# Prompt sparse attention: value products in the two PSUM halves, probability sums on Pool

## The chip, the cores and the metric

The kernel runs on one core of a Trainium2 chip. The metric is the device time of one execution in microseconds (us). The core's engines work side by side and meet at semaphores: TensorE (PE, matrix products into the eight banks ps of PSUM; PEld are its weight loads), VectorE (DVE), ScalarE (ACT), GpSimd (POOL) and SyncE (SP, here for transfers). Pool cannot read PSUM.

## The reference

One inference step of a hybrid decoder layer for a prompt group of 1024 tokens and a sample group of 8 x 4 tokens: input projection, RWKV-7 mixing, causal pooling, sparse attention, merging, cross-attention to 256 memory tokens, and an MLP. The change touches the sparse attention of the prompt alone. It has 8 query heads of 64 in 2 kv groups (4 heads share the keys and values of a group) and three branches:

```
lc = q . kc * scale + bias; pc = masked_softmax(lc);  o_cmp = pc . vc   # 16 block means
ls = q . ks * scale + bias; ps = masked_softmax(ls);  o_slc = ps . vs   # selected blocks of 64
lw = q . kw * scale + bias; pw = masked_softmax(lw);  o_win = pw . vw   # window of 512 keys
o = gate0 * o_cmp + gate1 * o_slc + gate2 * o_win
```

The prompt has 16 blocks and 16 are selected, so the selected branch sees every key up to the query's own position. The window branch sees the last 512. Both softmaxes need, for each query and head, a maximum, a sum of the exponentials and the product of the exponentials with the values.

## The kernel before, in words

The kernel is a chain of stages, each a block with one written program for each engine; a stage starts when the one before it has ended on all engines. `stage_nsa_prompt` is one of them. Its work is cut into 16 units: query tile i (128 tokens, i = 0 to 7) times kv group g, unit u = 2i + g. A unit has "tiles" of 128 keys: i + 1 of kind "s" (selected) and min(i, 4) + 1 of kind "w" (window), 2 to 13 a unit, 132 in all. G counts tiles over all units, k within one.

For a tile, `scores(G)` on TensorE writes 128 keys x (4 heads x 128 queries) into bank G % 2 with two products: L2152 (high parts of the keys) and L2153 (low parts, and a row that subtracts the maximum). Near the diagonal and at the window's edge, VectorE (`biased`, L2286) adds a bias into the ring PT, `np_probsT`, of four slots (NPT), and ScalarE takes the exponential there (L2357); for the other tiles ScalarE reads the bank itself (L2362). Two tiles later `values(G)` on TensorE (L2164) multiplies with the values, in plain fp32. The values have a 65th column of ones, so that row 64 of the result is the sum of the exponentials. Selected tiles add up in bank 2, window tiles in bank 3.

The rest of a unit is woven between the tiles of the next one by `plan(u)`. `look(u + 1, c)` computes scores the other way round for the maxima of the next unit (L2124, and L2120 for the edge; the form "cmp" at L2114 gives the scores of the block means), and VectorE's `see` reduces them (L2249, L2253). Looks use banks 4 and 5 in turn: look C waits until look C - 2 is seen. The form "cmpT" (L2117) turns the weights of the block means after VectorE's chain L2260 to L2267. `shift` (L2134) turns the negated maxima, in bank 7. After a unit's last tiles ScalarE evacuates both sums of products into OT (L2374), `turn` transposes them into banks 6 and 7 (L2173), VectorE's `scale` divides by the sums and multiplies by the gates (L2293 to L2299), `final` turns back and adds the block-mean branch (L2183, L2184), and `final_out` on ScalarE stores into oC (L2383). Pool only issues one gather at the stage's start (L2441).

Other places in the kernel are named by the prediction: L3608 in the cross-attention of the samples (`sample_values`: for each of four batches two products with 32 weight columns, into partitions 32b to 32b + 31 of one bank), L2617 and L2609 in the sample attention (a product with 32 weight columns, and transposes), L799, L811 and L816 in the RWKV preparation, and L1398 and L1942, elementwise work of Pool.

## Time and profile before

| | |
|---|---|
| time, median of 3 runs | 3045.2 us (3043.39 to 3047.57) |
| time of the profiled execution | 3039.11 us |
| its span | 3036.9 us |
| busy over the span | PE 2730.9, PEld 2440.2, DVE 1156.6, ACT 795.2, POOL 163.7 us |
| stage of the change | from 994.7 to 1343.6 us of the span: 348.9 us |
| mean granted TensorE clock | 0.94 of full over the span, 0.92 in the stage |

The span is the part of the profiled execution between its first and last instruction; 2.2 us lie around it. Times within the trace are counted from the span's start. A "record" is one line of TensorE's trace; an fp32 product has two, each with a weight load of its own. Record lengths overlap, because TensorE is a pipeline: the distance between two starts is what a record costs.

### The profile page before, as it was taken

What the parts mean: (1) busy time and instruction counts of PE and PEld (TensorE: products, weight loads), DVE (VectorE), ACT (ScalarE), POOL (GpSimd) and SP (SyncE); (2) the same over time, 40 slices, a digit from 0 to 9 for tenths busy, and PEclk for the clock granted to TensorE, in tenths of its full rate; (3) what the DMA queues carried; (4) which work ended last, traced back from release to release, by engine and by line L of the source; (5) the groups of instructions that cost most, each with busy time, mean ns of one, the idle gap of its engine ahead of it and who ended that gap; (6) DMA issues with size and microseconds to landing.
All of it is one profiled execution on the core that took longest, in us unless ns stands there. A gap on an engine that the chain in (4) does not pass through costs nothing. (4 is left out here: it accounts for less than half of the span.)

```text
span 3036.9 us, 49131 instructions
## 1 busy us (share of the span) xinstructions
PE 2730.9 (90%) x21538; PEld 2440.2 (80%) x21538; DVE 1156.6 (38%) x2020; ACT 795.2 (26%) x1245; POOL 163.7 (5%) x215
## 2 busy tenths in 40 slices
PE   5898588887997789987899999999889999999999
PEld 4897488873996455553689999999679999999998
DVE  4433644426052555634421333433444222222223
ACT  3223322211114334432221221221433212222112
POOL 1000222201211000012000000000000000000000
PEclk7999799987998699998999999998989999999999
DMA  4610100004530000027611111401301111111111
GB/s 164 235 42 15 17 3 3 3 4 149 114 86 4 18 1 1 1 104 253 264 46 49 46 42 53 126 26 35 118 21 49 43 49 49 42 49 42 49 49 65
DMA packets 178933, 192.09 MB, mean 63 GB/s; under 512 B 18214, under 2 KB 162897, under 8 KB 173624
## 3 DMA queue, kind: packets, MB, share of 16 engines
q1 hardware_dynamic: 168665, 127.05, 14.2%
q0 software_dynamic: 9888, 61.87, 5.9%
q8 instruction: 170, 2.79, 0.4%
q14 instruction: 42, 0.34, 0.0%
q10 hardware_dynamic: 168, 0.04, 0.0%
HBM read 165.28 MB, written 28.00 MB: 64 GB/s over the span
## 5 line engine op out<-in xcount | busy, mean ns | idle before, releaser
L3386 PE MATMUL ps<-ff_hidden_high,ff_high 128*128 128x352 f32 x768 | 247.7, 323 | 0.0
L3387 PE MATMUL ps<-ff_hidden_low,ff_high 128*128 128x352 f32 x768 | 246.7, 321 | 0.0
L3388 PE MATMUL ps<-ff_hidden_high,ff_low 128*128 128x352 f32 x768 | 246.4, 321 | 0.0
L586 PE MATMUL ps<-xf_h,ff_high 128*128 128x352 f32 x720 | 232.3, 323 | 2.0 <-DVE ff_low L575 2.0
L587 PE MATMUL ps<-xf_l,ff_high 128*128 128x352 f32 x720 | 230.8, 321 | 0.0
L588 PE MATMUL ps<-xf_h,ff_low 128*128 128x352 f32 x720 | 230.7, 320 | 0.0
L2986 PE MATMUL ps<-xn_h,me_gate_w_high 128*128 128x352 f32 x576 | 186.8, 324 | 4.9 <-DVE me_gate_w_low L3052 4.9
L2987 PE MATMUL ps<-xn_l,me_gate_w_high 128*128 128x352 f32 x576 | 185.4, 322 | 0.0
L2988 PE MATMUL ps<-xn_h,me_gate_w_low 128*128 128x352 f32 x576 | 185.2, 322 | 0.0
L3495 DVE TENSOR_TENSOR x<-x,ps 128x1056 f32<-128x1056 f32 x64 | 80.3, 1254 | 224.9 <-PE ps L3388 224.9
L3489 DVE TENSOR_TENSOR ff_hidden_low<-ff_act,ff_hidden_high 128x1056 fp32r<-128x1056 f32 x32 | 40.3, 1258 | 307.1 <-ACT ff_hidden_high L3461 307.1
L3386 PEld LDWEIGHTS ps<-ff_hidden_high,ff_high 128*128 128x128 f32 x768 | 144.2, 188 | 0.3 <-issue 0.3
L3387 PEld LDWEIGHTS ps<-ff_hidden_low,ff_high 128*128 128x128 f32 x768 | 144.3, 188 | 0.0
L3388 PEld LDWEIGHTS ps<-ff_hidden_high,ff_low 128*128 128x128 f32 x768 | 144.1, 188 | 0.0
L3438 ACT ACTIVATE ff_high<-ff_raw 128x1024 fp32r<-128x1024 f32 x63 | 66.3, 1053 | 294.3 <-PE ps L3388 286.7
L2164 PE MATMUL ps<-np_probsT,values_ones 128*65 128x512 f32 x264 | 140.0, 614 | 0.0
L586 PEld LDWEIGHTS ps<-xf_h,ff_high 128*128 128x128 f32 x720 | 135.1, 188 | 2.3 <-DVE ff_low L575 2.3
L587 PEld LDWEIGHTS ps<-xf_l,ff_high 128*128 128x128 f32 x720 | 135.3, 188 | 0.0
L588 PEld LDWEIGHTS ps<-xf_h,ff_low 128*128 128x128 f32 x720 | 135.0, 187 | 0.0
L586 PE MATMUL ps<-xn_h,pj_high 128*128 128x352 f32 x336 | 110.4, 328 | 7.6 <-DVE pj_low L575 7.6
L2986 PEld LDWEIGHTS ps<-xn_h,me_gate_w_high 128*128 128x128 f32 x576 | 108.7, 189 | 5.1 <-issue 5.1
L588 PE MATMUL ps<-xn_h,pj_low 128*128 128x352 f32 x336 | 109.7, 326 | 0.0
(699 smaller groups left out, 6435.5 us busy)
## 6 DMA issues: line engine op xcount, KB each, us to landing
ff_raw<-in_w_ff SPq DMA_DIRECT2D x64, 512.0 KB, 4.0
me_gate_w_raw<-in_w_in SPq DMA_DIRECT2D x23, 512.0 KB
pj_raw<-in_w_in SPq DMA_DIRECT2D x13, 512.0 KB, 4.2
xn_high<-xn_h POOLq DMA_DIRECT2D x1, 4224.0 KB, 12.1
xn_low<-xn_l POOLq DMA_DIRECT2D x1, 4224.0 KB, 24.1
xn_h<-xn_high POOLq DMA_DIRECT2D x1, 4224.0 KB, 15.9
xn_l<-xn_low POOLq DMA_DIRECT2D x1, 4224.0 KB, 26.2
xn_h<-xn_high SPq DMA_DIRECT2D x1, 4224.0 KB, 13.2
```

What stands on the lines that cost most here:

```text
L586: e.matmul(o, W.hi[:, z, k, :], rh[:, k, n], start=k == ks[0], stop=False)
L587: e.matmul(o, W.hi[:, z, k, :], rl[:, k, n], start=False, stop=False)
L588: mm = e.matmul(o, W.lo[:, z, k, :], rh[:, k, n], start=False, stop=k == ks[-1])
L2164: e.matmul(K.ps[0:65, 2 + z, :], va[:, z, j, g, :], PT[:, G % NPT, :], start=first, stop=j == i).then_inc(s_val, 1)
L2986: e.matmul(K.ps[:, c, 0:NW], wh[:, z, k, :], xh[:, k, chunk(c)], start=k == 0, stop=False)
L2987: e.matmul(K.ps[:, c, 0:NW], wh[:, z, k, :], xl[:, k, chunk(c)], start=False, stop=False)
L2988: mm = e.matmul(K.ps[:, c, 0:NW], wl[:, z, k, :], xh[:, k, chunk(c)], start=False, stop=k == KD - 1)
L3386: e.matmul(o, W.hi[:, u % NSPL, 2 * k + z, :], hh[:, r, ns], start=k == 0, stop=False)
L3387: e.matmul(o, W.hi[:, u % NSPL, 2 * k + z, :], hl[:, r, ns], start=False, stop=False)
L3388: mm = e.matmul(o, W.lo[:, u % NSPL, 2 * k + z, :], hh[:, r, ns], start=False, stop=k == GB - 1)
L3438: e.activation(W.hi[:, u % NSPL, :, :], W.raw[:, u % NRAW, :, :], ACT.Copy).then_inc(W.s_hi, 1)
L3495: e.tensor_tensor(c3(x[:, m, :]), c3(x[:, m, :]), bank(n), ALU.add).then_inc(s_read_down, 1)
```

## The change

The order of tiles within a unit becomes: first the selected tiles that have no window tile with the same keys, then selected and window tile of the same keys in turn (60 pairs, 12 single selected tiles). The value product drops the column of ones; the selected product goes to partitions 0 to 63 of a bank and the window product to partitions 64 to 127 of the same bank, and the two are issued one behind the other after the score product two tiles past the second (`together`). Banks 2 and 3 now alternate by unit. One evacuation of 128 partitions and four transposes of 128 replace two of 65 and eight.

The sums are made elsewhere: Pool keeps a running sum of the exponential tiles in `acc` (a copy for a kind's first tile, an add with a drain ahead of it for the others), one for each kind and unit parity. `sums(u)` on TensorE then multiplies each of its eight 128 x 128 parts with one column of ones into bank 7. A ring slot is free only when both the value product and Pool's add are done. `sums`, `turn` and `final` of the unit before now stand at tile slots 2, 3 and 5 of a unit (turn 2 and final 4 before; in short units at the last slot). The looks of a slot but the first now stand behind the value products of the slot. The turned block-mean weights move to SBUF that the tail rows have used, with a wait for their storing.

```diff
@@ -2022,7 +2022,7 @@
                                        ALU.mult, ALU.mult).then_inc(s_qu, 1)
-def stage_nsa_prompt(nc, K, qT, kvt, kcd, va, vbd, kh, kl, near, nearT, cb, idx, sk, wk):
+def stage_nsa_prompt(nc, K, qT, kvt, kcd, va, vbd, kh, kl, near, nearT, cb, idx, sk, wk, spare_at):
     units = [(i, g) for i in range(NTI) for g in range(2)]
@@ -2031,7 +2031,8 @@
     NPT = 4
     def tiles(i):
-        return [("s", j) for j in range(i + 1)] + [("w", j) for j in range(max(0, i - 4), i + 1)]
+        first = max(0, i - 4)
+        return [("s", j) for j in range(first)] + [(kind, j) for j in range(first, i + 1) for kind in KINDS]
     def shade(i, kind, j):
         return "near" if j >= i - 1 else "edge" if kind == "w" and j == i - 4 else ""
@@ -2062,10 +2063,18 @@
     spot = [(u, k) for u in range(NU) for k in range(len(tiles(units[u][0])))]
     NG = len(spot)
+    def together(G):
+
+        u, k = spot[G]
+        kind, j = tiles(units[u][0])[k]
+        if kind == "w":
+            return [G - 1, G]
+        return [G] if j < max(0, units[u][0] - 4) else []
+
     def plan(u):
         n = len(tiles(units[u][0]))
-        at = {"shift": n - 2 if n >= 4 else n - 1, "turn": min(2, n - 1), "final": min(4, n - 1)}
+        at = {"shift": n - 2 if n >= 4 else n - 1, "sums": min(2, n - 1), "turn": min(3, n - 1), "final": min(5, n - 1)}
         look = [[] for _ in range(n)]
         if u + 1 < NU:
             L = looks(u + 1)
@@ -2082,17 +2091,18 @@
         QA = sb("query_parts", [P, 2, 8, P], F32R)
         QB = sb("query_shift", [P, 2, 512], F32R)
         PT = sb("probsT", [P, NPT, 512])
-        OT = sb("outT", [65, 2, 512])
+        OT, acc = sb("outT", [P, 512]), sb("prob_sums", [P, 2, 2, 512])
         O = sb("out", [P, 2, 4, 64])
         mx, nm = sb("maxes", [P, 2, 4, 2, 3]), sb("negmax", [P, 2, 4, 2])
         co = sb("coef", [P, 2, 4])
-        sc, cT = sb("cmp_scores", [P, 8, 16]), sb("cmpT", [P, 2, P])
+        sc, cT = sb("cmp_scores", [P, 8, 16]), nc.alloc_sbuf_tensor_at("np_cmpT", [P, 2, P], F32, offset=spare_at)
         cm, cs = sb("cmp_max", [P, 8]), sb("cmp_sum", [P, 8])
         block = ctx.enter_context(nc.Block())
         s_qh, s_ql, s_clear, s_qb, s_look, s_seen, s_nm, s_cr = (K.sem("np_" + x) for x in (
             "queries_high", "queries_low", "shift_cleared", "shift_ready", "looked", "seen", "max", "shift_turned"))
         s_sc, s_add, s_exp, s_val, s_evac, s_turn, s_scaled, s_fin, s_fe = (K.sem("np_" + x) for x in (
             "scores", "biased", "exps", "values", "values_out", "turned", "scaled", "final", "final_out"))
+        s_acc, s_sum = K.sem("np_probs_added"), K.sem("np_probs_summed")
         s_ca, s_ce, s_cp = (K.sem("np_cmp_" + x) for x in ("shifted", "exps", "weighted"))
         @block.tensor
@@ -2159,18 +2169,24 @@
                 z = KINDS.index(kind)
                 first = j == (0 if z == 0 else max(0, i - 4))
                 e.wait_ge(s_exp, G + 1)
-                if first and u >= 1:
-                    e.wait_ge(s_evac, 2 * (u - 1) + z + 1)
-                e.matmul(K.ps[0:65, 2 + z, :], va[:, z, j, g, :], PT[:, G % NPT, :], start=first, stop=j == i).then_inc(s_val, 1)
+                if first and u >= 2:
+                    e.wait_ge(s_evac, u - 1)
+                e.matmul(K.ps[64 * z:64 * z + 64, 2 + u % 2, :], va[:, z, j, g, 0:64], PT[:, G % NPT, :], start=first, stop=j == i).then_inc(s_val, 1)
+
+            def sums(u):
+                e.wait_ge(s_qb, done["shift"])
+                e.wait_ge(s_acc, gbase[u + 1])
+                for a in range(4):
+                    for z in range(2):
+                        mm = e.matmul(K.ps[:, 7, 2 * a + z:2 * a + z + 1], acc[:, u % 2, z, P * a:P * a + P], K.c("ones")[:, 0:1], start=True, stop=True)
+                mm.then_inc(s_sum, 1)
             def turn(u):
-                e.wait_ge(s_evac, 2 * u + 2)
+                e.wait_ge(s_evac, u + 1)
                 if u >= 1:
                     e.wait_ge(s_fe, u)
-                e.wait_ge(s_qb, done["shift"])
-                for z in range(2):
-                    for a in range(4):
-                        mm = e.transpose(K.ps[:, 6 + z, 65 * a:65 * a + 65], OT[:, z, P * a:P * a + P], ident[0:65, 0:65])
+                for a in range(4):
+                    mm = e.transpose(K.ps[:, 6, P * a:P * a + P], OT[:, P * a:P * a + P], ident)
                 mm.then_inc(s_turn, 1)
                 done["turn"] += 1
@@ -2192,18 +2208,24 @@
                 for k in range(len(when)):
                     G = gbase[u] + k
                     scores(G)
-                    for c in when[k]:
+                    for c in when[k][:1]:
+                        look(u + 1, c)
+                    if G >= 2:
+                        for V in together(G - 2):
+                            values(V)
+                    for c in when[k][1:]:
                         look(u + 1, c)
                     if k == at["shift"] and u + 1 < NU:
                         shift(u + 1)
-                    if G >= 2:
-                        values(G - 2)
+                    if k == at["sums"] and u >= 1:
+                        sums(u - 1)
                     if k == at["turn"] and u >= 1:
                         turn(u - 1)
                     if k == at["final"] and u >= 1:
                         final(u - 1)
             values(NG - 2)
             values(NG - 1)
+            sums(NU - 1)
             turn(NU - 1)
             final(NU - 1)
@@ -2235,6 +2257,8 @@
                 elif form == "cmpT":
                     if i >= 2:
                         e.wait_ge(s_fin, 2 * i - 2)
+                    if i == 0:
+                        e.wait_ge(K.out_sem("tail_stored"), 16 * K.tail_stores)
                     e.tensor_copy(cT[:, i % 2, :], o[:, 0:P]).then_inc(s_seen, 1)
                 elif form == "edge":
                     for a in range(4):
@@ -2282,6 +2306,7 @@
                 e.wait_ge(s_sc, G + 1)
                 if G >= NPT:
                     e.wait_ge(s_val, G - NPT + 1)
+                    e.wait_ge(s_acc, G - NPT + 1)
                 by = nearT[:, j - i + 1, 4 * g:4 * g + 4, :] if how == "near" else K.c("edgeT").unsqueeze(1).to_broadcast([P, 4, P])
                 e.tensor_tensor(PT[:, G % NPT, :].rearrange("p (h n) -> p h n", h=4), K.ps[:, G % 2, :].rearrange("p (h n) -> p h n", h=4), by,
                                 ALU.add).then_inc(s_add, 1)
@@ -2289,14 +2314,15 @@
             def scale(u):
                 i, g = units[u]
                 e.wait_ge(s_turn, u + 1)
-                got = K.ps[:, 6:8, 0:260].rearrange("p z (a d) -> p z a d", a=4)
-                e.reciprocal(co[:, :, :], got[:, :, :, 64])
+                e.wait_ge(s_sum, u + 1)
+                got = K.ps[:, 6, :].rearrange("p (a z d) -> p z a d", a=4, z=2)
+                e.reciprocal(co[:, :, :], K.ps[:, 7, 0:8].rearrange("p (a z) -> p z a", z=2))
                 e.drain()
                 e.tensor_tensor(co[:, :, :], co[:, :, :], kvt[:, i, 776:KVG].rearrange("p (z h) -> p z h", z=2)[:, :, 4 * g:4 * g + 4], ALU.mult)
                 e.drain()
                 if u >= 1:
                     e.wait_ge(s_fin, u)
-                e.tensor_tensor(O[:, :, :, :], got[:, :, :, 0:64], co[:, :, :].unsqueeze(3).to_broadcast([P, 2, 4, 64]),
+                e.tensor_tensor(O[:, :, :, :], got, co[:, :, :].unsqueeze(3).to_broadcast([P, 2, 4, 64]),
                                 ALU.mult).then_inc(s_scaled, 1)
             e.tensor_scalar(QB[64:128, :, :].rearrange("p b (h n) -> p (b h) n", n=P),
@@ -2359,19 +2385,19 @@
                     e.wait_ge(s_sc, G + 1)
                     if G >= NPT:
                         e.wait_ge(s_val, G - NPT + 1)
+                        e.wait_ge(s_acc, G - NPT + 1)
                     e.activation(PT[:, G % NPT, :], K.ps[:, G % 2, :], ACT.Exp).then_inc(s_exp, 1)
             def evacuate(G):
                 u, k = spot[G]
                 i, g = units[u]
                 kind, j = tiles(i)[k]
-                if j != i:
+                if j != i or kind != "w":
                     return
-                z = KINDS.index(kind)
                 e.wait_ge(s_val, G + 1)
                 if u >= 1:
                     e.wait_ge(s_turn, u)
-                e.activation(OT[:, z, :], K.ps[0:65, 2 + z, :], ACT.Copy).then_inc(s_evac, 1)
+                e.activation(OT[:, :], K.ps[:, 2 + u % 2, :], ACT.Copy).then_inc(s_evac, 1)
             def cmp_exps(i):
                 e.wait_ge(s_ca, i + 1)
@@ -2418,6 +2444,20 @@
         def _(e):
             e.wait_ge(K.out_sem("tail_stored"), 16 * K.tail_stores)
             gather(e, sk[:, :], K.d["cache_slc_k"], idx, 0).then_inc(K.out_sem("s_keys_near"), 16)
+            for G in range(NG):
+                u, k = spot[G]
+                i, g = units[u]
+                kind, j = tiles(i)[k]
+                z = KINDS.index(kind)
+                to = acc[:, u % 2, z, :]
+                e.wait_ge(s_exp, G + 1)
+                if j == (0 if z == 0 else max(0, i - 4)):
+                    if u >= 2:
+                        e.wait_ge(s_sum, u - 1)
+                    e.tensor_copy(to, PT[:, G % NPT, :]).then_inc(s_acc, 1)
+                else:
+                    e.drain()
+                    e.tensor_tensor(to, to, PT[:, G % NPT, :], ALU.add).then_inc(s_acc, 1)
         @block.sync
         def _(e):
@@ -4207,7 +4247,7 @@
                 s_keys = nc.alloc_sbuf_tensor_at("s_keys_even", [P, SLOTS * P], F32, offset=low.tail)
                 s_window = nc.alloc_sbuf_tensor_at("s_window_keys_even", [P, 4, P], F32, offset=utail_at)
                 low.small = utail_at + 2048
-                stage_nsa_prompt(nc, K, qT, kvt, kcd, va, vbd, kh, kl, near, nearT, cb, idx, s_keys, s_window)
+                stage_nsa_prompt(nc, K, qT, kvt, kcd, va, vbd, kh, kl, near, nearT, cb, idx, s_keys, s_window, low.tail + SLOTS * P * 4)
             reuse_semaphores()
             merge_first = nc.alloc_sbuf_tensor_at("merge_gate_w_first", [P, KD, P], F32, offset=low.x + 2 * KD * T * 4)
             stage_sample_attn(nc, K, kvt, qT, ksn, kwn, idx, s_keys, s_window, low, ((flat(xh3), K.xh_dram), (flat(xl3), K.xl_dram)), merge_first)
```

## Rows read from the trace of the kernel before

**Rows 1.** Stage: us; PE, PEld, DVE, ACT, POOL busy; clock; DMA share, GB/s.

```profile
994.70:1343.60 348.90, 304.97 (x1382) 188.82 (x1381) 191.67 (x650) 134.51 (x248) 0.00 (x0) 0.92 0.01 3
```

**Rows 2.** The same view cut by unit: units 1, 10 and 15.

```profile
1013.90:1028.40 14.50, 11.62 (x41) 7.96 (x41) 6.96 (x28) 3.46 (x7) 0.00 (x0) 0.62 0.00 1
...
1191.50:1212.90 21.40, 21.00 (x94) 12.20 (x92) 14.01 (x43) 10.08 (x19) 0.00 (x0) 1.00 0.00 1
...
1313.20:1343.60 30.40, 26.84 (x103) 14.89 (x102) 6.28 (x12) 11.90 (x21) 0.00 (x0) 0.94 0.00 1
```

**Rows 3.** Whom TensorE waited for in the stage: us in total, times, longest.

```profile
PE ps L2117 <- DVE np_cmp_scores L2267: 15.4, 7, 2.5
PE ps L2124 <- DVE np_maxes L2249: 8.2, 12, 1.2
PE ps L2124 <- DVE np_maxes L2253: 6.0, 6, 1.5
```

**Rows 4.** Timeline of TensorE, last unit: start, us, engine, line, operation, count.

```profile
1314.59 1.02 PE L2164 MATMUL ps<-np_probsT,values_ones 128*65 128x512 f32 x2
...
1315.68 0.39 PE L2153 MATMUL ps<-np_query_shift,keys_low 128*128 128x512 f32 x1
1315.91 1.02 PE L2164 MATMUL ps<-np_probsT,values_ones 128*65 128x512 f32 x2
```

**Rows 5.** Timeline of TensorE, cross-attention, four 32-column products.

```profile
2164.24 1.94 PE L3608 MATMUL ps<-mm_s_values,mm_s_probsT 128*32 128x512 f32 x16
2166.01 1.89 PE L3593 MATMUL ps<-mm_s_keysT,mm_s_queries 128*32 128x256 f32 x8
```

**Rows 6.** Timeline of TensorE, sample attention, 32-column product between full-width transposes.

```profile
1357.34 1.05 PE L2617 MATMUL ps<-sa_keys_turned,sa_queries 128*32 128x512 f32 x2
1358.32 0.66 PE L2609 MATMUL ps<-cst,sa_keys_odd 128*128 128x128 f32 x4
1358.90 1.04 PE L2617 MATMUL ps<-sa_keys_turned,sa_queries 128*32 128x512 f32 x2
```

**Rows 7.** Timeline of TensorE, the shift's two-column products in unit 14.

```profile
1311.92 0.40 PE L2153 MATMUL ps<-np_query_shift,keys_low 128*128 128x512 f32 x1
1312.25 1.03 PE L2134 MATMUL ps<-cst,np_negmax 128*2 128x128 f32 x8
1313.21 1.07 PE L2164 MATMUL ps<-np_probsT,values_ones 128*65 128x512 f32 x2
```

**Rows 8.** Timeline of TensorE, the compressed scores' 16 records, at two clocks.

```profile
1014.88 3.43 PE L2114 MATMUL ps<-kcd,np_query_parts 128*128 128x16 f32 x16
...
1085.80 1.85 PE L2114 MATMUL ps<-kcd,np_query_parts 128*128 128x16 f32 x16
1087.50 1.04 PE L2124 MATMUL ps<-keys_high,np_query_parts 128*128 128x256 f32 x4
```

**Rows 9.** Pool's elementwise work by line: duration ns min/median/max, first and last start.

```profile
L1398 POOL TENSOR_TENSOR rs_Mn<-rs_M_RB,cst x80: 718/727/1173, 340.3 to 625.9; 128x256 f32<-128x256 f32 x80
...
L799 POOL TENSOR_TENSOR oB<-oB,oA x3: 2411/3432/3446, 314.6 to 320.4; 128x1056 f32<-128x1056 f32 x3
...
L1942 POOL COPY values_ones<-kvt x2: 1049/1052/1055, 961.1 to 962.1; 128x1024 f32<-128x1024 f32 x2
```

**Rows 10.** Timeline of VectorE while Pool ran L799's three.

```profile
319.31 2.25 DVE L816 TENSOR_TENSOR xs<-xs,rw_inv 128x1056 f32<-128x1056 f32 x1
321.48 1.30 DVE L811 SCALAR_TENSOR_TENSOR oA<-xs,par,ps 128x1056 f32<-128x1056 f32 x1
```

**Rows 11.** Timeline of VectorE, the compressed weights before a turn.

```profile
1286.57 0.29 DVE L2267 TENSOR_TENSOR np_cmp_scores<-np_cmp_scores,np_cmp_sum 128x128 f32<-128x128 f32 x1
```

**Rows 12.** Timeline of the stage's last steps, all engines.

```profile
1334.59 0.63 ACT L2357 ACTIVATE np_probsT<-np_probsT 128x512 f32<-128x512 f32 x1 [0.69 <-DVE np_probsT L2286]
...
1337.08 0.71 PE L2173 MATMUL ps<-cst,np_outT 65*128 65x65 f32 x8 [0.68 <-ACT np_outT L2374]
...
1339.10 1.22 PE L2183 MATMUL ps<-cst,np_out 128*128 128x128 f32 x4 [1.31 <-DVE np_out L2299]
```

## The prediction

> **What bounds the kernel now.** I first cut the span into three stretches with the table of windows. The stage that the diff touches takes 348.9 us; TensorE is busy for 305 of them, VectorE for 192, ScalarE for 135, Pool for none [rows 1]. So TensorE is the engine to follow, and Pool is free. Cut by unit (a unit is one query tile and one kv group), the table shows two regimes [rows 2]. Unit 10 takes 21.4 us with TensorE busy for 21.0 at full clock: there every TensorE pass removed is time gained. Unit 1 takes 14.5 us with 11.6 busy at a mean clock of 0.62: there a chain over three engines sets the pace. The list of waits says which: 15.4 us in 7 waits for the compressed weights, 14.2 us in 18 waits for the row maxima [rows 3].
>
> The timeline of the last unit gives the price of a tile: one value product starts every 1.32 us; between L2153 and the next L2164 lie 0.23 us [rows 4]. A score product is one record, a value product two ("x2"). With 0.23 for each of the two score products, the value product costs 1.32 - 0.46 = 0.86 us, 0.43 a record. It has 65 output columns, so half of the array is idle in it.
>
> **The change part by part.** There are 132 tiles: 60 pairs (one selected and one window tile of the same keys) and 12 single selected tiles, in i = 5, 6, 7.
>
> *Pairs.* Do two products with the same 128 rows, in two column halves, run together? The stage doesn't show it. The nearest rows do: L3608 sends four batches, each two 512-wide fp32 products, to four 32-column strips, batch after batch in the program. The 16 records last until the next line starts 1.77 us later [rows 5]. Serial they would take 16 x 0.43 = 6.9 us; four deep they take 4 x 0.43 = 1.7. So the strips run side by side although their instructions come one batch after the other. I take full overlap: a pair costs 0.86 instead of 1.72.
>
> *Changing the array's form.* In the sample attention a 32-column product (two records, 0.86) and four 128-wide transposes repeat every 1.56 us, and the transposes take 0.43 (the four are 16/4 of the 0.107 that a 128-column record costs, below): 1.56 - 0.86 - 0.43 = 0.27 is left for going into the narrow form and back [rows 6]. The shift gives 0.10 in (0.33 against 0.23) and 0.11 out (0.96 against 8 x 0.107) [rows 7]. Bounds 0.21 and 0.27, plus a little for loads of 64 columns; I take 0.25, nearer to rows 6, where a 512-wide product goes in as it does here. Pairs: 60 x (1.72 - 0.86 - 0.25) = -36.6 us. Singles: 12 x 0.25 = +3.0.
>
> The Trainium skill (TensorEngine Tiling (Array Packing), Key Properties) says that changing the tiling mode drains the engine. By that rule and the rows alike, all 72 visits pay.
>
> *Where the saving doesn't count.* 20 of the 60 pairs lie in i <= 3, where TensorE has idle time (2.9 us in unit 1, 0.4 in unit 10 [rows 2]); with the looks packed into the first tile slots, VectorE sets the pace there, and a shorter TensorE only waits longer. Half of 20 x 0.61 is given back: +6.1 (bounds 0 and 12).
>
> *Sums on TensorE.* Eight fp32 products a unit load 128 x 128 weights twice each for one moving column. L2114 is that shape with 16 moving columns: 16 records in 1.70 us at full clock, 0.107 each, and 3.43 at half [rows 8]. 16 units: 15 inside the stage, 15 x 1.70 = +25.5; the 16th is in the tail. The 7 in i <= 3 fall partly into waits that are there anyway: -4 (bounds 0 and -12). At half clock the first ones cost up to 1.7 more each, while pairs there save more: +1.7.
>
> *Sums on Pool.* 32 copies and 100 adds of 512 columns. A copy of 1024 takes 1.05, so 0.52. An add of 256 took 0.73, the 1056-wide ones 2.41 to 3.45 [rows 9], which scale to 1.17, 1.46 and 1.67. I take 1.3 and 0.1 for the drain ahead of it. A unit of 13 tiles then costs Pool 2 x 0.5 + 11 x 1.4 = 16.4 us. Unit 14 has about 24 us for that, and the last unit 3 x (0.46 + 0.86 + 0.25) + 5 x (0.92 + 0.86 + 0.25) + 3.4 for sums, turn and final = 18.3 us. So Pool hides, by 8 us and by 2. The sums product stands at the third tile of the next unit, some 4 us behind the last score product, and the last add ends about 3 us behind it: no wait. If that cover goes, TensorE stops there with scores, looks and values queued behind it, and through the ring of four ScalarE's exponentials stop too.
>
> *The read port.* While Pool added, L816 with two operands in SBUF took 2.25 us, and L811 of the same width with one of them in PSUM 1.30 [rows 10]; Pool's own times rose from 2.41 to 3.43. The chain that TensorE waits for 7 times has three such operations, 0.29 us each when long [rows 11]. If about half of an add falls on it each time, 7 x 0.6 = +4 (bounds 0 and 25, three whole adds each time). The near maxima and the biases read PSUM and stay as they are.
>
> *Tail.* Now the last exponential ends at 1335.22 and the turn starts at 1337.08 [rows 12]. After: Pool's add ends 1.4 behind the exponential, values have the array until 1.0 and leave it, eight sum products take 1.7, then the turn: at 3.1 to 3.7 instead of 1.9, +1.5 (bound 3).
>
> *Turn and final.* Four transposes of 128 for eight of 65: 4 x 0.107 against 0.46, nothing. The final moves to the slot after next; in the two units of four tiles both now stand in the same slot, so that TensorE waits for VectorE's scaling, 1.31 as in the tail [rows 12]: 2 x 1.3 = +2.6 (bound 0).
>
> *Looks around values, one evacuation instead of two, the extra waits.* Looks after the first now have a value pair between them, which can fill waits from i = 2 on: -2 (bounds 0 and -8). Evacuations fall from 32 to 16 on ScalarE, which is busy for 39% and hides them. Every second slot has no values, but the score product two on needs an exponential that started over 1.3 us before. Pool's wait for the tail rows was over before the stage; VectorE's new wait on the same semaphore comes later still: nothing.
>
> **Sum.** -36.6 + 3.0 + 6.1 + 25.5 - 4 + 1.7 + 4 + 1.5 + 2.6 - 2 = +1.8 us. Against the profiled execution, 3039.1, that gives 3040.9; the median of the runs is 3045.2, 6.1 higher, so 3047.0. What this kernel's measurement can tell from no change is 0.2%, 6.1 us: I forecast no change, because the passes saved by pairing are bought back by weight loads for the sums.
>
> **Rivals.**
> *Faster.* The give-back (6.1), the wait for scaling (2.6) and the port (4) don't appear, and the looks fill 6 instead of 2: 1.8 - 16.7 = -14.9, 3030. For it: units 8 to 15 are full of TensorE work, and there alone 40 x 0.61 - 3.0 - 8 x 1.70 = 7.8 us are gained. Against: the waits of rows 3 end on VectorE, which gets no faster. 0.25.
>
> *Slower: Pool's add is the bound.* Place: the ring of four and the sums. It decides from (18.3 - 1)/11 = 1.57 us an add in the last unit and about 2.1 in units 8 to 14. With 2.1, the last unit loses 6, and with a wait of 1 to 1.5 at 11 sums 14 more: +22, 3067. For it: 1.67 is among the scaled rows, and a drain's cost isn't shown. Against: those long adds were beside a two-operand VectorE operation. 0.12.
>
> *Slower: starts in program order.* If a strip's product couldn't start before the ones ahead of it have started, a pair's four records A A B B would overlap in one place only: 3 x 0.43 + 0.25 = 1.54, saving 0.18 each, 10.8 instead of 36.6. With 4.3 less to give back, 1.8 + 25.8 - 4.3 = +23: 3068. 0.07, since rows 5 would then last 13 x 0.43 = 5.6 us. The Trainium skill (TensorE: Matmul & The Clock Gate, Part 3: Packing small matmuls) calls matmuls strictly first in, first out in start and end, which is this case; rows 5 speak against it. No overlap at all, the change not doing what it says, would be 36 us more; 0.02.
>
> *Slower: port or form.* Each compressed chain meets two adds (+14 in place of +4), or each visit costs 0.35 (+7): 3054 to 3057. 0.10.
>
> **How the numbers follow.** No change 0.44; faster 0.25; slower 0.12 + 0.07 + 0.02 + 0.10 = 0.31. The predicted time is the first case's, 3047, with its own range 3039 to 3052. The range takes in the faster rival and most of the port and Pool cases: 3030 to 3063; outside stay order, no overlap, and half of the ends.
>
> **What would show it.** The value records of a pair starting within 0.1 us of each other, and the next line 0.86 + 0.15 later; 128 sum products, 1.7 us a unit; Pool busy for some 150 us, adds at 1.2 to 1.4; units 8 to 14 shorter by about 1 us each, units 1 to 7 not shorter; L2267 longer than 0.29 when Pool runs. I am wrong if the visits cost much else than 0.25, if Pool's adds pass 1.6, or if the early units follow TensorE's work after all.

## The result and the profile after

The changed kernel takes 3089.32 us (median of 4 runs, 3084.28 to 3104.18) against 3044.3 for the kernel before on the same chip: ratio 1.0159, 95% interval 1.0143 to 1.0174. It is slower by 1.6%. The forecast was no change, with 3063 as the upper end of the range.

The windows of the changed kernel, cut where the stage's first load is issued and where the next stage's is (us; then busy time of PE, PEld, DVE, ACT, POOL; clock; DMA share, GB/s):

```profile
0.00:987.42 987.42, 806.88 (x10288) 722.85 (x10288) 417.05 (x628) 250.79 (x463) 127.52 (x177) 0.90 0.22 64
987.42:1388.13 400.71, 341.02 (x1576) 208.56 (x1576) 206.88 (x654) 129.41 (x237) 148.08 (x133) 0.82 0.01 4
1388.13:3087.20 1699.07, 1616.03 (x9866) 1526.16 (x9866) 544.99 (x738) 406.42 (x529) 35.46 (x37) 0.97 0.23 75
```

Cut in the same way, the stage before took 352.4 us ([rows 1] start 3.5 us later). So 48.3 us are lost in the stage. Outside it the two profiled executions differ by 2 us in all (3.8 less ahead of the stage, 5.8 more behind it). The third column from the end is the row's message: the granted clock fell from 0.92 to 0.82. The clock has two levels, half (1.2 GHz) and full (2.4 GHz), so a mean of c over T us is 2 x (1 - c) x T at half: 56 us before, 144 after. At half clock a record costs about twice its price (a value product below takes 1.84 us there and 0.95 at full clock). The forecast charged 1.7 us for sum products that meet half clock, and took it for given that the clock itself stays.

Units 1, 3, 10 and 15 of the changed kernel, same columns; [rows 2] are units 1, 10 and 15 before:

```profile
1009.48:1025.87 16.39, 12.19 (x41) 7.83 (x41) 7.85 (x29) 2.87 (x6) 1.23 (x2) 0.50 0.00 1
1044.18:1074.62 30.44, 22.91 (x89) 15.73 (x89) 11.92 (x41) 5.12 (x10) 4.53 (x5) 0.61 0.00 1
1221.13:1245.42 24.29, 24.03 (x106) 13.64 (x106) 14.83 (x43) 10.05 (x19) 11.12 (x10) 0.85 0.00 1
1354.20:1388.13 33.93, 29.02 (x125) 15.38 (x124) 6.00 (x12) 10.76 (x19) 18.50 (x16) 0.86 0.00 0
```

Unit 10, which had been full of TensorE work at full clock in 21.4 us, is again full of it but takes 24.3, at 0.85. Unit 3 took 21.3 before, at 0.79, so it alone lost 9 us.

The list of waits of TensorE in the stage after (total us, times, longest) answers to [rows 3]:

```profile
PE ps L2127 <- DVE np_cmp_scores L2291: 27.1, 8, 4.7
PE ps L2134 <- DVE np_maxes L2273: 11.4, 23, 1.1
PE ps L2199 <- DVE np_out L2325: 5.2, 4, 1.3
PE ps L2124 <- DVE np_query_parts L2238: 4.4, 1, 4.4
PE ps L2181 <- ACT np_query_shift L2375: 4.1, 3, 2.8
...
PE ps L2181 <- POOL np_prob_sums L2460: 2.0, 1, 2.0
PE ps L2134 <- DVE np_maxes L2277: 1.8, 3, 0.8
```

The first wait, for the compressed weights (of the block means), was 17.8 us in 8 times before in the same cut; the 4.4 us once, at the stage's start, stood there before too. In TensorE's timeline a pair of value products looks like this (start, us, engine, line, records):

```profile
1241.64 0.45 PE L2162 MATMUL ps<-np_query_parts,keys_high 128*128 128x512 f32 x1
1241.92 0.40 PE L2163 MATMUL ps<-np_query_shift,keys_low 128*128 128x512 f32 x1
1242.25 1.08 PE L2174 MATMUL ps<-np_probsT,values_ones 128*64 128x512 f32 x4
1243.26 0.51 PE L2162 MATMUL ps<-np_query_parts,keys_high 128*128 128x512 f32 x1
1243.60 0.40 PE L2163 MATMUL ps<-np_query_shift,keys_low 128*128 128x512 f32 x1
```

Four records share 1.01 us, so the halves run side by side. But from the start of L2163 to the second start of L2163 are 1.68 us; less two score products at 0.23, the pair cost 1.22, which is 0.86 and 0.36 for the form. The score product behind it needs 0.34 to its next start in place of 0.23: that last 0.11 is the part of leaving the narrow form that the forecast did not count. At full clock all 17 pairs that stand between two score products in this trace have a median of 0.33 in, 1.01 and 0.34.

VectorE and Pool in the stage after, by line (count, busy us, mean ns; idle time before them); lines between them are left out:

```profile
L2286 DVE TENSOR_TENSOR np_cmp_scores<-np_cmp_scores,cst 128x128 f32<-128x128 f32 x8 | 5.7, 708 | 0.6
L2289 DVE TENSOR_TENSOR np_cmp_sum<-np_cmp_sum,kvt 128x8 f32<-128x8 f32 x8 | 4.6, 574 | 0.6
L2291 DVE TENSOR_TENSOR np_cmp_scores<-np_cmp_scores,np_cmp_sum 128x128 f32<-128x128 f32 x8 | 4.3, 531 | 0.6
L2457 POOL COPY np_prob_sums<-np_probsT 128x512 f32<-128x512 f32 x32 | 20.0, 625 | 98.7 <-ACT np_probsT L2383 84.9 <-ACT np_probsT L2389 13.8
L2460 POOL TENSOR_TENSOR np_prob_sums<-np_prob_sums,np_probsT 128x512 f32<-128x512 f32 x100 | 127.3, 1273 | 144.8 <-ACT np_probsT L2383 90.5 <-ACT np_probsT L2389 49.6 <-issue 4.6
```

Last, a place where the clock falls, in unit 7:

```profile
1150.97 1.34 PE L2134 MATMUL ps<-keys_high,np_query_parts 128*128 128x256 f32 x4 [0.33 <-DVE np_maxes L2273]
1152.15 2.18 PE L2181 MATMUL ps<-cst,np_prob_sums 128*128 128x1 f32 x16
1154.19 0.77 PE L2162 MATMUL ps<-np_query_parts,keys_high 128*128 128x512 f32 x1
1154.76 0.63 PE L2163 MATMUL ps<-np_query_shift,keys_low 128*128 128x512 f32 x1
1155.19 0.41 PE L2134 MATMUL ps<-keys_high,np_query_parts 128*128 128x256 f32 x1
1155.53 1.98 PE L2174 MATMUL ps<-np_probsT,values_ones 128*64 128x512 f32 x4
```

Behind the sixteen one-column records of L2181 (2.04 us to the next start, where 1.70 is the length of 16 such loads at full clock [rows 8]) a pair of values takes 1.91 us in place of 1.01.

### The profile page after: what moved, and what is told of

Same layout as the page of the kernel before. It is cut to its first block and busy times, and to the rows that moved or that the text cites. A ratio compares the mean times of both kernels' runs of the same rounds, so it can differ in the third digit from the quotient of the medians.

```text
span 3087.2 us, 49774 instructions
## 1 busy us (share of the span) xinstructions
PE 2763.9 (90%) x21730; PEld 2457.6 (80%) x21730; DVE 1168.9 (38%) x2020; ACT 786.6 (25%) x1229; POOL 311.1 (10%) x347
## 5 line engine op out<-in xcount | busy, mean ns | idle before, releaser
L2460 POOL TENSOR_TENSOR np_prob_sums<-np_prob_sums,np_probsT 128x512 f32<-128x512 f32 x100 | 127.3, 1273 | 144.8 <-ACT np_probsT L2383 90.5
## 6 DMA issues: line engine op xcount, KB each, us to landing
xn_h<-xn_high SPq DMA_DIRECT2D x1, 4224.0 KB, 13.2
```

What stands on the lines that cost most here:

```text
L2460: e.tensor_tensor(to, to, PT[:, G % NPT, :], ALU.add).then_inc(s_acc, 1)
```

## The experiments

Each ratio is to the kernel before, run on the same chip in the same session (its medians there: 3043.25 for e1 to e4, 3043.96 for e5 to e8, 3044.39 for e9 to e12 and 3044.15 for e13 to e16). "Profiled" is the time of the one profiled execution, "stage" the length between the same two loads in it, with its granted clock. The profiled execution is not the median: it was 12 us below it for e7_rows_hold, 4 to 6 below it for the kernel before and e12_tiles, and above it by 11 for e5_hold, 6 for e1_no_pool and 4 for e8_order. Outside the stage the profiled executions take from 2679 (e7_rows_hold) to 2696 us (e5_hold), so a stage is compared with a stage, and a median with a median.

| run | median us | ratio (95% interval) | profiled us | stage us | clock |
|---|---|---|---|---|---|
| before | | 1 | 3039.11 | 352.4 | 0.92 |
| after | 3089.32 | 1.0159 (1.0143 to 1.0174) | 3089.70 | 400.7 | 0.82 |
| e1_no_pool | 3072.07 | 1.0081 (1.0055 to 1.0108) | 3078.49 | 384.4 | 0.82 |
| e2_dense_sums | 3072.49 | 1.0095 (1.0078 to 1.0112) | 3074.32 | 382.6 | 0.87 |
| e3_one_sum | 3067.71 | 1.0080 (1.0063 to 1.0097) | 3066.49 | 375.6 | 0.83 |
| e4_neither | 3035.37 | 0.9981 (0.9971 to 0.9991) | 3036.02 | 345.2 | 0.88 |
| e5_hold | 3076.93 | 1.0102 (1.0080 to 1.0124) | 3087.46 | 389.8 | 0.82 |
| e6_rows | 3072.09 | 1.0093 (1.0076 to 1.0110) | 3074.28 | 382.6 | 0.85 |
| e7_rows_hold | 3054.79 | 1.0041 (1.0027 to 1.0055) | 3042.84 | 361.7 | 0.89 |
| e8_order | 3030.77 | 0.9958 (0.9944 to 0.9972) | 3034.92 | 348.3 | 0.90 |
| e9_late_pairs | 3055.22 | 1.0035 (1.0025 to 1.0046) | 3055.89 | 364.6 | 0.87 |
| e10_no_pairs | 3083.73 | 1.0132 (1.0115 to 1.0150) | 3082.85 | 391.2 | 0.89 |
| e11_looks | 3037.47 | 0.9986 (0.9974 to 0.9998) | 3036.75 | 348.3 | 0.91 |
| e12_tiles | 3040.55 | 0.9985 (0.9972 to 0.9997) | 3036.42 | 348.8 | 0.92 |
| e13_order_fill | 3031.93 | 0.9964 (0.9951 to 0.9977) | 3031.27 | 341.9 | 0.93 |
| e14_after_fill | 3073.85 | 1.0106 (1.0087 to 1.0124) | 3072.64 | 387.1 | 0.85 |
| e15_rows_hold_fill | 3040.05 | 0.9988 (0.9978 to 0.9998) | 3041.97 | 352.0 | 0.93 |
| e16_order_thin | 3036.62 | 0.9982 (0.9973 to 0.9992) | 3034.60 | 348.8 | 0.91 |

### Taking out Pool's work, the sum products, or both

No Pool (the sums are products with a tile of ones; the probability sums are left out):

```diff
-            for G in range(NG):
...
-                    e.tensor_tensor(to, to, PT[:, G % NPT, :], ALU.add).then_inc(s_acc, 1)
+            e.memset(acc[:, :, :, :], 1.0).then_inc(s_acc, 1)
```

> Leaves out Pool's copies and adds; Pool sets the sums buffer to ones once, so the selected and window outputs are divided by a wrong number. The products, sums products and order of the changed kernel stay. Theory P (read port and Pool): VectorE's operations with two SBUF operands no longer meet Pool, the waits of the weights' turn fall from 27.1 us back to 15 to 16, TensorE no longer idles for over 4 us before it, and most of the 45 us go: 3045 to 3055. Theory C (clock by the sums products): weight loads with one moving column leave TensorE without work that keeps its clock, so the granted clock in the stage stays below 0.86 and the time at 3070 to 3080.

Dense sums, two products of ones with 512 columns a unit, of about the same length; what they compute is not the sum for each query:

```diff
-                for a in range(4):
-                    for z in range(2):
-                        mm = e.matmul(K.ps[:, 7, 2 * a + z:2 * a + z + 1], acc[:, u % 2, z, P * a:P * a + P], K.c("ones")[:, 0:1], start=True, stop=True)
+                for z in range(2):
+                    mm = e.matmul(K.ps[:, 7, :], K.c("ones"), acc[:, u % 2, z, :], start=True, stop=True)
```

> Replaces the eight one-column sums products of a unit (16 weight loads of 128 columns, 1.7 us) by two fp32 products of 512 moving columns (2 x 0.86 = 1.7 us): the same time on TensorE at full clock, but full of columns. Scaling then reads the sums in the wrong layout, so the selected and window outputs are wrong. Theory C: the clock no longer falls at the sums, mean clock in the stage 0.88 or more, time 3055 to 3065. Theory P: nothing changes, 3085 to 3092, clock 0.82.

One small sum product a unit in place of eight (the divisors are then wrong), and the same without Pool:

```diff
+                mm = e.matmul(K.ps[:, 7, 0:8], acc[:, u % 2, 0, 0:P], K.c("ones")[:, 0:8], start=True, stop=True)
```

> One sums product of eight columns a unit in place of eight of one column, so 1.5 us less a unit on TensorE and wrong divisors for the selected and window outputs; Pool's adds stay. Theory C: 24 us of loads go and the clock with them, another 20 to 30: 3035 to 3045. Theory P: only the loads go, 3060 to 3068, and the waits of the weights' turn stay at 25 us or more.

> Both of the above: no adds on Pool and one sums product a unit, so wrong divisors for the selected and window outputs. What is left is the pairing, the order, the looks and the later turn and final. By the prediction's terms (-36.6 + 3.0 + 6.1 + 2.6 - 2 and 2 for the single product left) 3044 - 25 = 3019, clock as before, 0.92. If pairing itself lowers the clock (half as many column passes as time), 3035 or more with a clock below 0.88.

The two suspects share the loss. Pool costs 0.78% (24 us) with the sum products there and 0.99% (30) with only one; the sum products cost 0.79% (24) beside Pool and 1.0% (30) without it; both together 1.78% (54). Of the sum products' 24 to 30 us, 16 x (1.70 - 0.24) = 23.4 are their own length at full clock (0.24 is the small product in e4_neither), which the forecast had. What is left, order and pairs, gains only 0.19% (6 us), where the forecast's terms for it (pairs, singles, give-back, scaling, looks) come to -26.9. Dense sums of the same length as the thin ones are 0.64% faster (20 us), at 0.87 for 0.82.

Against what was expected: e1 fell in the range of theory C, but the wait for the weights did go back to 19.5 us, as theory P says in kind. e2 missed both ranges: the clock rose, to 0.87 and not 0.88, and the time fell only to 3072.5. e3 went as theory P said, 3067.7 with a wait of 30.2 us: without seven of the eight thin products the clock rose only to 0.83, so these products alone do not explain it. e4 missed the 3019 of the forecast's terms by 16 us; at 3035.4 and 0.88 it is close to its other case. So neither theory held alone, and both causes were followed up.

### Holding Pool back, and other sums

Pool waits ahead of the shift's slot in the odd units until the compressed weights are done:

```diff
+                if g == 1 and i + 1 < NTI and k == plan(u)[0]["shift"] - 1:
+                    e.wait_ge(s_cp, i + 2)
```

> The changed kernel with one wait more: in the odd units Pool's adds stop one tile ahead of the shift until the compressed weights are done, so that no add of Pool lies beside VectorE's three two-operand operations of that chain. Same work, same output. Port theory (adds beside the chain lengthen it, and the seven waits of TensorE behind it set the half clock off): the three operations go back from 0.71, 0.57 and 0.53 to about 0.3, 0.2 and 0.3 us, the waits for the turn of the weights fall from 27.1 us to 16 to 20, and the time falls by 10 to 20 us, to 3070 to 3079. Clock theory (one-column sum products and not the chain lower the clock): the operations get shorter, but the time stays within 6 us of 3089.

The sums as rows:

```diff
-                        mm = e.matmul(K.ps[:, 7, 2 * a + z:2 * a + z + 1], acc[:, u % 2, z, P * a:P * a + P], K.c("ones")[:, 0:1], start=True, stop=True)
+                    mm = e.matmul(K.ps[32 * z:32 * z + 32, 7, :], K.c("ones")[:, 0:32], acc[:, u % 2, z, :], start=True, stop=True)
...
+                e.wait_ge(s_row, u + 1)
+                for a in range(4):
+                    mm = e.transpose(K.ps[:, 7, 64 * a:64 * a + 64], rowsT[:, P * a:P * a + P], ident[0:64, 0:64])
...
+                e.activation(rowsT[:, :], K.ps[0:64, 7, :], ACT.Copy).then_inc(s_row, 1)
```

> The changed kernel with the probability sums made another way, same output: per unit two products with 32 weight columns of ones against all 512 columns of the sums, into two column strips of bank 7 side by side, ScalarE copies these rows, and four more transposes turn them. In place of 64 records of one to a few columns there are 4 records of 512 and 8 of 64 columns or so, about 1.5 us in place of 1.7 a unit. Clock theory (few-column products leave TensorE counted as idle, and the clock falls behind them): like the dense sums, which gave 3072.5, or a few us less: 3062 to 3074, with the granted clock of the stage at 0.86 to 0.88. Port theory: the chain of the compressed weights is as long as before (waits of about 27 us stay), and the time stays within 8 us of 3089.

> Both edits together: sums as rows of 512 columns and Pool held back from the compressed chain. If the two losses are separate and add, it is 10 to 20 us below the run with rows alone: 3045 to 3060. If Pool costs the stage in another way than by this chain (the run without Pool's adds but with dense sums would then be the only way back), the two runs with rows agree within 6 us.

With Pool held back, VectorE's lines in e5_hold (columns as above) read:

```profile
L2286 DVE TENSOR_TENSOR np_cmp_scores<-np_cmp_scores,cst 128x128 f32<-128x128 f32 x8 | 2.3, 293 | 0.6
L2291 DVE TENSOR_TENSOR np_cmp_scores<-np_cmp_scores,np_cmp_sum 128x128 f32<-128x128 f32 x8 | 2.3, 293 | 0.9 <-issue 0.4
L2289 DVE TENSOR_TENSOR np_cmp_sum<-np_cmp_sum,kvt 128x8 f32<-128x8 f32 x8 | 1.3, 168 | 0.6
```

These are the lengths without Pool (292, 293 and 167 ns in e1_no_pool). The wait for the weights is 19.5 us for 27.1, and the time is 0.57% (17 us) lower, most of what leaving Pool out altogether gives (0.78%; the rest is within the intervals). So Pool's adds cost mostly by where they lie, not by their number: the port theory holds. Two larger groups of VectorE say the same: the adding of the bias, which reads PSUM, takes 689 ns before (L2286) and after (L2311), and the splitting of the queries, with two SBUF inputs, went from 686 (L2216) to 848 (L2238). The rows give 0.66% (20 us), as much as the dense sums, and 0.61% on top of the hold: the two losses are separate and add. All three times fell where the theories that won had put them; the clock of e6_rows, 0.85, is a little below its 0.86 to 0.88.

### Order alone, and pairing alone

The kernel before with the new order of tiles and of looks and values:

```diff
-        return [("s", j) for j in range(i + 1)] + [("w", j) for j in range(max(0, i - 4), i + 1)]
+        first = max(0, i - 4)
+        return [("s", j) for j in range(first)] + [(kind, j) for j in range(first, i + 1) for kind in KINDS]
...
-                    for c in when[k]:
+                    for c in when[k][:1]:
                         look(u + 1, c)
-                    if k == at["shift"] and u + 1 < NU:
-                        shift(u + 1)
                     if G >= 2:
                         values(G - 2)
+                    for c in when[k][1:]:
+                        look(u + 1, c)
+                    if k == at["shift"] and u + 1 < NU:
+                        shift(u + 1)
```

> The kernel before with nothing but the new order of tiles (selected and window tile of the same keys next to each other) and the new order of looks and values inside a tile slot; the value products keep 65 columns and nothing is paired, the slots of turn and final stay as they were. The run with pairs and this order, without sums and Pool, was at 3035.4, 8 us below before, where 25 were forecast for these parts. If the order itself costs (a pair of slots with looks and scores but one burst of values): 3050 to 3062, and the pairs give 15 to 25 us as forecast. If the order costs nothing: 3040 to 3047, and the pairs themselves give only 5 to 10 us, because their saving goes into waits for VectorE.

The lower half of that diff alone, then the upper half alone:

> The kernel before with only the order inside a tile slot changed: the first look ahead of the value product, the others and the shift behind it; the tiles stay in the old order (all selected, then all window). Both parts together gave 3030.8, 13 us below before, where 2 were forecast. If the gain is cover for the waits (a value product between the looks and ahead of the shift): 3030 to 3034. If it comes from the order of the tiles: 3041 to 3045.

> The kernel before with only the order of tiles changed (selected and window tile of the same keys next to each other), looks and shift ahead of values as before. Complement of the run on the order of looks: 3041 to 3045 if the looks' order is what gains, 3030 to 3034 if the tiles' order is (the biased near tiles are then spread in twos instead of coming in two bursts).

The order alone is 0.42% below before (13 us); no kernel of this study is faster. Both cases of its expectation were above it. Each half gives 0.14 or 0.15%, with intervals that reach to 0.02 and 0.03%, so neither of the two expectations held; they add to most of it. Of the 13 us the profiled executions show only 4, all in the stage: the one of the kernel before was 5 us below the session's median, that of the order alone 4 above its own. So the other 9 us lie between these executions and the medians and can't be placed.

Now the run with pairs but without Pool and sums, with the two products of a pair put one behind the other, in i = 1 to 3 and then in i = 1 to 7 (they go to the same 64 columns; the accumulation is left out as well; the diff is that of the second):

```diff
-                e.matmul(K.ps[64 * z:64 * z + 64, 2 + u % 2, :], va[:, z, j, g, 0:64], PT[:, G % NPT, :], start=first, stop=j == i).then_inc(s_val, 1)
+                h = j % 2 if i >= 1 else z
+                e.matmul(K.ps[64 * h:64 * h + 64, 2 + u % 2, :], va[:, z, j, g, 0:64], PT[:, G % NPT, :], start=first or i >= 1, stop=j == i or i >= 1).then_inc(s_val, 1)
```

> From the run without Pool's work and with one small sum product a unit (3035.4; its output is not complete, as the sums are left out). Here both value products of a pair in i = 1 to 3 go to the same 64 columns, so that they run one after the other (each starts its own sum; what they accumulate is left out); i = 4 to 7 keep their pairs. 18 of the 60 pairs are serial, which is 18 x 0.86 = 15.5 us more TensorE work. Theory of pairing as forecast (half of it counts): 3035.4 + 8 = 3043. Theory that the early units follow VectorE and that shorter TensorE work there only lets the clock fall: the early units come back to those of the order alone (unit 4: 21.5 us for 25.8, unit 5: 18.2 for 21.9), granted clock of the stage 0.90 for 0.88, and 3035.4 or below, down to 3028.

(That text counts units from one: its unit 4 is unit 3 here.)

> The same with the value products serial in all of i = 1 to 7: 58 of 60 pairs serial, all else as in that run. The difference between the two is the price of pairing alone: forecast was 60 x 0.86 saved with half of a third given back, so 3035.4 + 40 = 3075 if the saving counts (the form is changed either way). If the early units give nothing: 40 late pairs x 0.86 = +34, 3069. If even late pairs go into waits: 3040 to 3055.

A serial pair in e10_no_pairs:

```profile
1290.42 0.39 PE L2163 MATMUL ps<-np_query_shift,keys_low 128*128 128x512 f32 x1
1290.74 1.93 PE L2175 MATMUL ps<-np_probsT,values_ones 128*64 128x512 f32 x4
1292.60 0.50 PE L2162 MATMUL ps<-np_query_parts,keys_high 128*128 128x512 f32 x1
1292.93 0.40 PE L2163 MATMUL ps<-np_query_shift,keys_low 128*128 128x512 f32 x1
```

1.86 us where the true pair had 1.01: 0.85 saved for a pair, as forecast. The 58 pairs then give 46.0 us of stage and 1.51% (46 us) of time, of 58 x 0.86 = 49.9. The 18 early ones give 19.5 us of stage and 16 of time, the 40 late ones 26.6 and 29.5 (of 15.5 and 34.4). Both runs came out above all their expectations (3043 and 3075 were the highest). My theory that the early units follow VectorE is wrong: units 2 to 7 alone, where the 18 lie, grew by 13.2 us. Pairing itself does nearly all that its price says. Yet the serial version is 53 us (1.74%) above the order alone, though its value products have the same number of columns to stream: this is what the 64-column form and the rest of the change bring with them, taken up below.

### Work in the waits

TensorE's waits for the compressed weights (form "cmpT"), seven from i = 1 on, filled with ten products of 512 columns, whose result is overwritten:

```diff
+                    for _ in range(10 if i else 0):
+                        e.matmul(o[:, :], QA[:, i % 2, 0, :], kh[:, 0, g, 0:512], start=True, stop=True)
                     e.wait_ge(s_cp, i + 1)
```

> The fastest version so far (the kernel before with the new order of tiles, looks and values, 3030.8) with work added: ahead of each wait for the compressed weights, from i = 1 on, ten products of 512 columns into the free look bank, whose result is overwritten (0.23 us each at full clock, 2.3 us in seven places, 16 us in all). Theory of the clock (the half clock follows these idle stretches): the waits of 18.8 us fall to 3 to 6, the half-clock time of the stage falls, granted clock 0.94 or more for 0.90, 3018 to 3027. Theory of work (only work and waits count): the added products lie in a wait that is there anyway, or reach past it, so 3030 to 3038.

> The changed kernel as it is with the same ten products at the same seven places. Clock theory: 3089 falls by 10 to 30 us, to 3060 to 3079, and the granted clock of the stage rises from 0.82 to 0.86 or more; what is left is what the few-column sum products do to it. Theory of work: 3087 to 3095.

> The best version with pairs (sums as rows, Pool held back from the compressed chain, 3054.8) with the same ten products at the same seven places. Clock theory: 3035 to 3048, granted clock 0.93 or more for 0.89 in the stage. If so pairing comes near the kernel before, but stays above the order alone, since 72 changes of form at 0.36 and the sums cost more than the 60 x 0.86 that it saves. Theory of work: 3052 to 3062.

And with products in the shape of the sums:

```diff
+                    for _ in range(11 if i else 0):
+                        e.matmul(o[:, 0:1], QA[:, i % 2, 0, :].bitcast(F32), K.c("ones")[:, 0:1], start=True, stop=True)
```

> As the first of these four, but the time is filled with eleven products of one moving column and 128 columns of weights each (the shape of the sum products of the changed kernel, two records each at 0.107, 2.35 us) in place of ten of 512 columns. If few-column products leave TensorE as good as idle for the clock: no gain over 3030.8, or a loss, 3029 to 3040, with the clock at 0.90 or below. If any work in the wait keeps the clock: the same time as the run with products of 512 columns, within 4 us.

The same place in unit 9, first idle (e8_order), then with dense work (e13_order_fill), then with thin work (e16_order_thin):

```profile
1181.93 0.45 PE L2118 MATMUL ps<-cst,np_cmp_scores 128*128 128x128 f32 x1 [2.55 <-DVE np_cmp_scores L2270]
1182.17 1.92 PE L2165 MATMUL ps<-np_probsT,values_ones 128*65 128x512 f32 x2
1184.02 1.46 PE L2135 MATMUL ps<-cst,np_negmax 128*2 128x128 f32 x8
```

```profile
1181.31 2.50 PE L2118 MATMUL ps<-keys_high,np_query_parts 128*128 128x512 f32 x10
1183.95 0.33 PE L2120 MATMUL ps<-cst,np_cmp_scores 128*128 128x128 f32 x1
1184.11 1.02 PE L2167 MATMUL ps<-np_probsT,values_ones 128*65 128x512 f32 x2
1185.06 1.03 PE L2137 MATMUL ps<-cst,np_negmax 128*2 128x128 f32 x8
```

```profile
1182.08 2.70 PE L2118 MATMUL ps<-cst,np_query_parts 128*128 128x1 f32 x22
1184.71 0.47 PE L2120 MATMUL ps<-cst,np_cmp_scores 128*128 128x128 f32 x1
1184.98 1.92 PE L2167 MATMUL ps<-np_probsT,values_ones 128*65 128x512 f32 x2
1186.82 1.43 PE L2137 MATMUL ps<-cst,np_negmax 128*2 128x128 f32 x8
```

and unit 9 as a whole in windows, dense, then thin:

```profile
1162.33:1186.13 23.80, 23.66 (x116) 15.28 (x116) 14.97 (x50) 8.93 (x17) 0.00 (x0) 1.00 0.00 0
```

```profile
1163.09:1188.30 25.21, 25.21 (x128) 16.59 (x129) 14.96 (x50) 8.92 (x18) 0.00 (x0) 0.93 0.00 1
```

TensorE is busy throughout in both. Behind the dense work the values take 0.95 us to the next start, behind the thin work 1.84, twice as much, and behind 2.55 us of idling 1.85. With nothing in the wait the unit took 25.3 at 0.93, so in this place thin work is worth as much to the clock as none. Units 1 and 13 show the same (dense 0.73 and 1.00; thin and idle both 0.60 and 0.96); in unit 3 dense work made no difference (0.77 for 0.80 and 0.78), and in units 5, 7 and 11 the clock was full in all three.

In the changed kernel 16 us of added work make it 0.53% (16 us) faster, and 0.53% again on top of rows and hold, which brings a version with pairs to 0.9988, just below the kernel before. Both lie where the clock theory put them, though the clock of e14 is 0.85 and not 0.86. In e14 TensorE's busy time in the stage rose by only 4.2 us (345.2 for 341.0) with 16 us of work added. On the order alone the stage of the profiled execution is 6.4 us shorter at 0.93 for 0.90, but the runs show no gain (3031.93 against 3030.77); the expectation of 3018 to 3027 failed. Thin work in that place is 0.18% above dense work, with intervals that just touch, and 0.24% (7 us) above the order alone; its clock, 0.91, is a little above the 0.90 expected, and neither case of its expectation holds to the letter.

## Why the prediction was wrong

**What failed first: the sum has no term for the clock.** "128 sum products" were priced at the full clock of [rows 8], 25.5 us; that is right for a unit at full clock. The forecast took the clock of [rows 1], 0.92, for given and charged only 1.7 for the half clock early. Put the measured prices into its sum, against the stage before: pairs -51.6, forms 72 x 0.36 = +25.9, sums +25.5, tail +3.0, compressed chain +9.3 (27.1 - 17.8), row maxima -1.6 (13.2 for 14.8), scaling +2.6, waits of the sums for the shift +2.6 (4.1 for 1.5 at the turn before). That is +15.7. The stage lost 48.3, so 32.6 are left. The clock column gives (144 - 56) / 2 = 44 as the most that half clock can have added; part of it fell into idle time. Taken from the records, TensorE was busy for 46 us of its half-clock time before and for 122 after, and half of the difference is 38, near the 32.6. The shares of the stage agree: its busy time grew by 35.3 us (341.0 for 305.7), where the priced busy terms come to nothing, and its idle time by 13.0. That the clock is a cause and not a companion, e2, e6 and e14 show: the same length of work in dense form is 20 us faster, and added dense work shortens the kernel. What lowered it was not one thing: with one sum product in place of eight it was still 0.83, without Pool 0.82, without both 0.88.

The Trainium skill (TensorE: Matmul & The Clock Gate, Part 1: The HAM clock gate) says that the default is the throttled clock and that activity lifts it. The trace agrees: unit 1 of the changed kernel, with TensorE busy for 12.2 of 16.4 us, was at 0.50, and unit 10 before, busy for 21.0 of 21.4, at 1.00. In e16_order_thin, though, half clock followed 22 one-column records in a row as it followed an idle wait.

**Pairs: right in kind, the give-back wrong.** Full overlap held (1.01 us for four records). The four start in two couples, 0.48 us apart and within 0.01 in each, as the forecast's sign says, so the rival of starts in program order is out: the second product did not wait for the second record of the first. Of the 0.86 a pair 92% showed in the time. The +6.1 for i <= 3 was not there: e9 shows 16 to 19 us for 18 early pairs priced at 15.5. I had read VectorE's waits in [rows 3] as if the whole early unit followed them. The price of no overlap, "36 us more", is a slip: the visits would still be paid, so it is the 60 x 0.86 = 51.6 less the give-back of 6.1; the serial e10 was 46 us above e4.

**Form: mis-sized.** 0.36 a visit, not 0.25: 72 x 0.11 = +7.9. The 0.11 is in the score product behind the visit, and [rows 7] was read only to that product's start. The period in [rows 6] is whole and gave 0.27, for 32 columns between transposes; why a visit costs 0.36 here isn't shown. It is the rival "port or form", which had 0.35.

**Port: the place right, the size wrong.** L2286, L2289 and L2291 grew from 0.29, 0.17 and 0.29 to 0.71, 0.57 and 0.53: 1.06 a chain for my 0.6, and the waits by 9.3 for my 4. Holding Pool off the chain gives 17 us in the medians for 7.6 us of wait, so the longer wait costs about as much again through what comes behind it; the two profiled stages are 10.9 us apart, so part of this is not placed. The Trainium skill (SBUF — State Buffer, SBUF: two separate sides) calls the port of VectorE and Pool an exclusive lock for VectorE operations with two SBUF inputs; L2289, with 8 columns, bears this out: it went from 0.17 to 0.57 on average, with 1.11 as its longest, near a whole add of Pool (1.27).

**Pool's add as the bound: rejected.** 1.27 us and 0.16 of gap, 1.43 against the 1.57 from which it decides. VectorE waits for Pool once, 0.9 us, and TensorE in one place, the tail, 2.0: the turn stands 4.9 us behind the last exponential, +3.0 where I had +1.5 with 3 as the bound.

**Scaling:** 5.2 for 2.6 us, as forecast. **Looks and order:** forecast -2 for the looks and nothing for the order of tiles; the order alone is -4 in the stage of the profile and -13 in the runs.

**The balance of the change.** Pairing, as it has to be done here, is not a gain at all: -51.6 for the overlap, +25.9 for 72 changes of form, +28.5 for sums and tail, before Pool's cost to the chain and the clock: +2.8. The order gained what the whole change could keep.

**What stays open.** The serial version is 42.9 us of stage above the order alone. The forms (25.9), the small sum product (16 x 0.24 = 3.8), 7.4 more of idle TensorE time and half of its 86 - 70 = 16 us more at half clock (8) make 45. That is an addition of prices, not a run: the form was not tried without the rest. Why the clock is lower there (0.89 for 0.90), whether by the form or by the waits, was not tried alone. Nor was it settled why dense filling lifts the clock of the order alone without a gain in the runs; there the profiled execution of the order alone was 4 us above its median, that of the filled version 1 below, so most of the 6.4 us by which the stages differ may be chance.

## What to carry to other kernels

Before trading TensorE passes, look at the clock column of the stage: when it is below 1, ask what the change does to idle stretches and to products with few columns, and give that a term of its own. Price a change of form from the last start before it to the second start behind it, and ask what the narrow form makes necessary elsewhere. Work for Pool is nearly free by its busy time and dear by its place: keep it off short two-operand chains on VectorE that TensorE waits for. And test an order of issue alone: here it was the only part worth keeping.

## What the runs showed of the hardware

- Half clock followed twenty-two one-column fp32 records in a row as it followed 2.55 us of idling: 1.84 and 1.85 us for the next value product, 0.95 behind ten 512-column products of the same length.
- Added useless work made a kernel faster twice, by 16 us each, with 16 us of work added.
- A 64-column product among full-width ones costs 0.36 us more, of which 0.11 shows in the product behind it; two in a row pay once (1.86 for a serial pair, of which 1.72 are its four records). Two such products for the two halves, in a row, run side by side (1.01 for four records), and their records start in couples.
- An fp32 add of 512 columns on Pool takes 1.27 us, with 0.16 to the next behind a drain; with such adds about, an 8-column VectorE operation with two SBUF operands takes 0.57 us on average and up to 1.11, in place of 0.17.
